# The attention stage of a streaming encoder: where TensorE's spare transposes stand among scores and values

## The reference

```python
def fox_attend(q, k, v, fq, fk, qpos, kpos):
    s = jnp.einsum('bqkgd,bskd->bkgqs', q, k) * (FOX_DH ** -0.5)
    s = s + fq_ - fk[:, :, :, None, :]          # decay between query and key
    s = jnp.where(kpos[None, :] <= qpos[:, None], s, -jnp.inf)
    p = jax.nn.softmax(s, axis=-1)
    o = jnp.einsum('bkgqs,bskd->bqkgd', p, v)
...
    o = o.reshape(b, L, FOX_W) * jax.nn.silu(g)
    return x + gate[:, None, :] * (o @ w_out), ...
```

## Time and profile before

| | us |
|---|---|
| median of three runs | 1787.82 |
| the profiled execution, its own time | 1787.6 |
| its span, first to last instruction | 1785.8 |
| TensorE busy | 1719.3 |
| VectorE, ScalarE, GpSimd busy | 693.5, 564.4, 341.2 |
| the tail in that execution, from 1454 to the end | about 332 |

### The profile page before, as it was taken

How to read it: one execution, slowest core, us unless ns; L and a number is a source line. 1 busy time by engine, 2 the same in 40 slices (tenths; PEclk the granted TensorE clock), 3 DMA queues, 4 the chain that set the end, 5 groups by cost and what they waited for, 6 DMA issues and landing times.

```text
span 1785.8 us, 21820 instructions
## 1 busy us (share of the span) xinstructions
PE 1719.3 (96%) x8461; PEld 1325.1 (74%) x8461; DVE 693.5 (39%) x1421; ACT 564.4 (32%) x924; POOL 341.2 (19%) x409
## 2 busy tenths in 40 slices
PE   3699999999999999999999999999999998999998
PEld 0699998777876666666668888888788866777776
DVE  1654443111134344444533334744552115443432
ACT  2321111111133444444431224425222134344432
POOL 1311111100012222222232125415201000110000
PEclk9999999999999999999999999999999999999999
DMA  9064444452345656556562311332223635332200
GB/s 336 33 222 161 153 159 152 162 183 83 121 148 175 208 183 194 171 187 232 170 235 67 105 48 36 118 106 88 89 92 120 179 136 166 116 103 71 71 25 36
DMA packets 122136, 242.86 MB, mean 136 GB/s; under 512 B 15617, under 2 KB 50589, under 8 KB 121010
## 3 DMA queue, kind: packets, MB, share of 16 engines
q1 hardware_dynamic: 101282, 175.61, 30.7%
q0 software_dynamic: 20752, 65.86, 9.6%
HBM read 170.42 MB, written 70.99 MB: 135 GB/s over the span
## 4 chain that ended last, share of the span: by engine, by line
PE 94%; ACT 1%; DVE 1%; issue 1%; POOL 0%; DVEq 0%; ACTq 0%; POOLq 0%
PE trunk_ps L1053 39%; PE in_ps_o L538 11%; PE in_ps_o L534 11%; PE tail_ps L1906 6%; PE tail_ps L1897 4%; PE tail_ps L1864 3%; PE trunk_ps L1079 3%; PE trunk_ps L1094 3%; PE tail_ps L1874 2%; PE trunk_ps L1089 2%; PE trunk_ps L1155 1%; PE tail_ps L1840 1%; PE in_ps_o L559 1%; PE trunk_ps L1123 1%; PE trunk_ps L1066 1%; PE trunk_ps L1112 1%
## 5 line engine op out<-in xcount | busy, mean ns | idle before, releaser
L1053 PE MATMUL trunk_ps<-w_hi,hT_hi 128*128 128x512 f32 x1008 | 410.4, 407 | 0.0
L1053 PE MATMUL trunk_ps<-w_hi,hT_lo 128*128 128x512 f32 x1008 | 401.1, 398 | 0.0
L1053 PE MATMUL trunk_ps<-w_lo,hT_hi 128*128 128x512 f32 x1008 | 397.2, 394 | 0.0
L1053 PEld LDWEIGHTS trunk_ps<-w_hi,hT_hi 128*128 128x128 f32 x1008 | 189.3, 188 | 59.4 <-issue 17.5
L1053 PEld LDWEIGHTS trunk_ps<-w_lo,hT_hi 128*128 128x128 f32 x1008 | 189.5, 188 | 49.3 <-issue 5.0
L1053 PEld LDWEIGHTS trunk_ps<-w_hi,hT_lo 128*128 128x128 f32 x1008 | 189.2, 188 | 44.5
L203 DVE TENSOR_TENSOR w_lo<-w_raw,w_hi 128x1024 fp32r<-128x1024 f32 x80 | 101.4, 1270 | 298.1 <-ACT w_hi L191 292.2
L534 PE MATMUL in_ps_o<-hT_hi,w_hi 128*128 128x384 f32 x384 | 131.5, 342 | 4.7 <-DVE hT_lo L620 4.7
L534 PE MATMUL in_ps_o<-hT_hi,w_lo 128*128 128x384 f32 x384 | 130.0, 339 | 0.0
L534 PE MATMUL in_ps_o<-hT_lo,w_hi 128*128 128x384 f32 x384 | 130.0, 338 | 0.0
L538 PE MATMUL in_ps_o<-w_hi,hT_hi 128*128 128x512 f32 x288 | 114.4, 397 | 0.0
(11 more groups left out here) (240 smaller groups left out, 2649.7 us busy)
## 6 DMA issues: line engine op xcount, KB each, us to landing
w_raw<-in_a_w_in SPq DMA_DIRECT2D x96, 256.0 KB, 3.0
room<-in_state_ret SPq DMA_DIRECT2D x64, 256.0 KB, 4.0
out_state_sample<-room POOLq DMA_DIRECT2D x64, 256.0 KB, 4.7
room<-in_b_ada_w SPq DMA_DIRECT2D x24, 512.0 KB, 6.2
scratch_qkT<-room POOLq DMA_DIRECT2D x48, 192.0 KB, 2.2
scratch_v<-room POOLq DMA_DIRECT2D x36, 256.0 KB, 2.5
room<-scratch_v SPq DMA_DIRECT2D x36, 256.0 KB, 4.4
scratch_o<-room POOLq DMA_DIRECT2D x36, 256.0 KB, 3.6
```

The source lines that it names most:

```text
L1053: ins = pe.matmul(ps[:, bank, :], h[:, k, t * P:(t + 1) * P], w[:, (C0 + j) % 2, k, :], start=k + m == 0, stop=k == KT - 1 and m == 2)
```

## The change

Two pairs of statements change places, one pair on TensorE and one on VectorE. On TensorE the extras of a unit are issued before `values(u)`. On VectorE `low_part(s, i)` is issued before `output(u)`. Nothing is added or removed; ScalarE, GpSimd and the DMA queues keep their lists, and so does `ring`.

```diff
@@ -1918,9 +1918,9 @@
                 turn_weights(u)
                 if u + 2 < UNITS:
                     scores(u + 2)
-                values(u)
                 for key in extras(s, i):
                     turn(key)
+                values(u)
                 if s:
                     n0 = sum(COUNT[:i])
                     for c, h in ITEMS[n0:n0 + COUNT[i]]:
@@ -2115,9 +2115,9 @@
                 over_sum(u)
                 if u + 2 < UNITS:
                     softmax(u + 2)
-                output(u)
                 if s and i < 2:
                     low_part(s, i)
+                output(u)
                 if s == 0 and i % 2 == 0:
                     split_lo(pr, dve, C0 + 1, 1, i // 2)
```

## The result

The changed kernel takes 1771.95 us (median of six runs, 1767.10 to 1772.52) against 1786.45 us for the kernel before on the same occasions: a ratio of 0.9913, with a 95% interval of 0.9902 to 0.9925. By the profiled executions it is 1772.2 against 1787.6, so 15.4 us less, where 11.9 were forecast. The direction came out as forecast, and so did the places, but for units 8 and 9; the sum was 3.5 us short. Executions of one kernel lie several microseconds apart (1781.11 to 1788.79 before), so the single terms are read from the profiles.

A forecast was written before the change was run, and what follows sets the result against it. TensorE, busy 1719.3 of 1785.8 us, was taken as the bound, so only its idle gaps could count. Minus 6.2, plus 0.3, minus 1.0, 1.8 and 3.2 made minus 11.9: 1776 us, range 1774 to 1778, with rivals 1771.5 to 1783.

The forecast's parts named there:

- units 8 and 9: Step 1, units 0 and 1: longer VectorE chain and an expected fall of the granted clock, plus 0.3 us.
- steps 5 to 8: Second weight group of unit 1 waits less for `low_part`: 0.8 us, four times, minus 3.2 us.
- gaps ahead of the values in steps 1 to 4: Units 2 to 4 of each step: turns fill gaps of 0.33 to 0.35, 0.28, 0.17 and 0.06 us.
- first two units of steps 2 to 4: Second output turn waits for `low_part`, taking back most of the vanished gap: 0.1 us gained per step.
- Step 0: Earlier key turns bring `move`, cast and copy forward; unit 8 begins 6.2 us earlier: minus 6.2 us.
- minus 1.0 becomes plus 0.3: Up to unit 10's values: low clock makes work about 1.7 us longer, some 0.4 of it slack.
- a gain of 1.0 at full clock: Unit 8's start to unit 10's values: 8.1 us after the change against 9.1 before.
- Units 10 to 12 and steps 2 to 4: Turns fill gaps ahead of values: minus 1.0 us in step 1, minus 1.8 us in steps 2 to 4.
- (a): The clock does not fall in step 1: minus 1.3 us more, 1774.6 us; chance 0.18.
- (b): Step 0 gives only half, or the low clock lasts longer: 1779.1 us; chance 0.20.
- (c): Units 0 and 1, steps 1 to 4: TensorE waits for `output` behind `low_part`, 1.6 us each; 1791.2 us; chance 0.04.
- (d): No change: idle time only moves and ScalarE sets the pace, 1787 us; chance 0.05.

The follow-up runs named there:

- early load: Changed kernel with the load of step 1's values tile issued ahead of the last weight quarter: 1772.06 us, ratio 0.9924 to the kernel before.
- filler: Changed kernel with twelve and eight more identity transposes ahead of the values of units 8 and 9: 1768.95 us, ratio 0.9908 to the kernel before.
- query and key turns alone: Kernel before with TensorE's new order only at i of 2 and up in steps 1 to 8, VectorE as before: 1783.10 us, ratio 0.9976.
- last turn moved: Changed kernel with early load and the turn of the last step's first output half ahead of unit 71's values: 1771.93 us, ratio 0.9918 to before.
- no residual addition: Changed kernel without GpSimd's residual addition (line 2015), stores and semaphores kept: 1766.37 us in one run, its tail beginning 4.6 us earlier.
- step 0 alone: Kernel before with TensorE's new order in step 0 only, all else as before: 1781.95 us, ratio 0.9969.

## Where the prediction was right, and which steps failed

The mechanism was right: most of the gain is idle time of TensorE that the turns fill, and `low_part` ahead of `output` lets the weights of steps 5 to 8 go on. What failed are the sizes of four terms, which make nearly all of the 3.5 us. The stretch of units 8 and 9 has the wrong sign (1.1 us, the chain and the low clock both too dear). The gaps ahead of the values in steps 1 to 4 were priced at the gap or less, and a closed gap gives back more (1.0 us). The first two units of steps 2 to 4 were put at almost nothing for a wait that came in one step of three (0.7 us). In steps 5 to 8 `low_part` was started too late (0.6 us).

**Step 0 (forecast -6.2, measured -6.47).** Right, and by its own steps: `move` leads to the next scores, the cast stands ahead of the copy. Unit 2 began 1.26 us nearer to the start of the tail (forecast 1.27), units 4, 6 and 8 3.8, 4.6 and 6.5 us (forecast 3.7, 4.4 and 6.2). The residual gap of about half a microsecond in unit 5 is there (0.5 us, ahead of line 1888).

**Units 8 and 9 (forecast +0.3, measured -0.78).** The step that failed is the sum behind "minus 1.0 becomes plus 0.3". It counts from the start of unit 8 to the values of unit 10: 9.1 us before, 8.1 after at full clock, and 1.3 more for a fall of the clock (1.7 us of longer work less 0.4 of slack), so 9.4. The 9.1 is right, 1485.73 to 1494.81. In the changed kernel it was not 9.4 but 8.37, from 1479.38 to 1487.75. First in the kernel before, then in the changed one:

```profile
1494.81 0.46 PE L1897 MATMUL tail_ps<-room,tail_pT 128*128 128x128 f32 x2 [0.22 <-ACT tail_pT L1995]
```

```profile
1487.75 0.41 PE L1897 MATMUL tail_ps<-room,tail_pT 128*128 128x128 f32 x2
```

Both terms were too dear. The chain takes 7.64 us where the clock held (early load, 1478.40 to 1486.04; the same with filler), not 8.1. The fall of the clock then cost 0.73 us, not 1.3. One reason is the slack: with filler, at full clock, TensorE would have been ready for the values of unit 10 at about 1486.67 (an estimate, the turn's start at 1486.23 and its 0.44 us), and `output` let them start at 1487.39, so the slack is 0.7 us and not 0.4.

The words "a gain of 1.0 at full clock" set a chain at full clock against a kernel that was at 0.50 for 6.8 us of this stretch. That does not enter the sum, since 9.1 is what the kernel before took. But it hides that at full clock in both the new order gains nothing up to unit 10 (6.16 against 6.20 us from unit 8) and loses 0.4 up to unit 11. That the stretch came out at a gain is the clock's doing and in this sense luck: TensorE is at 0.50 from about 1487 to 1493.8 before and from 1483.6 to 1487 after, clock 0.91 instead of 0.83 over the same 20 us. The order of the chain was right: values of unit 9 wait for `output` (0.70 us), behind `low_part`:

```profile
1482.79 0.69 DVE L2093 TENSOR_TENSOR tail_oT_lo<-room,tail_oT_hi 128x512 fp32r<-128x512 f32 x1 [0.69 <-ACT tail_oT_hi L1973]
...
1483.40 0.34 DVE L2070 SCALAR_TENSOR_TENSOR tail_o<-tail_ps,tail_mx,tail_g 128x128 f32<-128x128 f32 x1
...
1483.80 0.80 PE L1897 MATMUL tail_ps<-room,tail_pT 128*128 128x128 f32 x2 [0.70 <-DVE tail_o L2070]
```

**Units 10 to 12 and steps 2 to 4 (forecast -1.0 and -1.8, measured -1.26 and -3.21).** The mechanism was right, two sizes were off. "A gap of 0.39 which a turn of 0.44 fills" was priced at 0.33 to 0.35. A turn that fills the gap gives back all of it, 0.39, and the quicker pair of values and turn 0.05 more, together about the 0.43 measured. In steps 2 to 4 the gaps were priced right (0.28, 0.17 and 0.06) and the 0.07 us beside each left out: 0.35, 0.24 and 0.14 measured. The query and key turns alone gave the same, 1.1 us in units 10 to 12 and 2.2 us in steps 2 to 4, where the forecast has 1.0 and 1.5. And for units 0 and 1 of steps 2 to 4 I took 0.1 us per step, since the second turn waits for `low_part`. That happened only in step 2 (0.78 us waited, 0.03 us gained in the pair); steps 3 and 4 gained 0.57 and 0.38. The -3.21 lies beyond the bound of -2.7 that the forecast gave for steps 2 to 4.

**Steps 5 to 8 (forecast -3.2, measured -3.8).** The mechanism is right: the turn leads, and `low_part` follows the softmax at once, here in step 5.

```profile
1589.33 0.08 DVE L2051 DVE_READ_ACCUMULATOR2_ANT tail_mx<- 128x1 f32 x1
1589.33 0.69 DVE L2093 TENSOR_TENSOR tail_oT_lo<-tail_ps,tail_oT_hi 128x512 fp32r<-128x512 f32 x1
1589.37 1.04 PE L1874 MATMUL tail_ps<-ident,tail_s_sb 128*128 128x128 f32 x5
...
1590.08 0.14 PEld L1874 LDWEIGHTS tail_ps<-ident,tail_s_sb 128*128 128x128 f32 x1 [0.35 <-DVE tail_oT_lo L2093]
```

The remaining wait is hidden within a merged group: step 5's weights take 0.87 us from start to start instead of 0.55, so 0.32 us, close to the 0.38 that the forecast leaves of 1.18. Only step 8's shows in the list, 0.20 us. The 0.6 us more than forecast come from the start of `low_part`, at least in step 5. The forecast put it at the end of the softmax's last record (1601.04 in the earlier trace rows); it started together with that record, 0.08 us sooner, and the fifth transpose followed its end by 0.06 us instead of 0.1 (1590.02 to 1590.08). So from unit 41's start to that transpose are 0.71 us, where the forecast has 0.84.

**The rivals.** (a) The clock fell in the changed kernel's profile and in that of the kernel with the last turn moved, but not in three others with this order in units 8 and 9 (early load, filler, no residual addition), so whether it does in a given run is open; it is worth 0.66 us there, not 1.3. (b) is refuted by step 0. (c), `output` behind `low_part` as the bound, is what VectorE's part does alone, 1.0016, at 0.4 to 0.7 us a step in steps 2 to 4 instead of 1.6 per place; beside TensorE's part it shows once. (d) is refuted. The load lay under VectorE's chain, as forecast; in the kernel with step 0 alone it did not.

What stays open: why the low stretch was shorter in the changed kernel, and what decides whether it comes. The kernel with the early load and the one with the last turn moved issue the same work up to unit 71, and the clock held in the first profile and fell in the second.

## What to carry to other kernels

Work that waits for nothing belongs between the request for a result and its use; first replay one unit from the traces' starts, and price a gap by the distance of the starts, not by the list of waits (0.39 against 0.22 us here; closed, it gave 0.43). Look at who frees the bank, since a filler that needs the result itself fills nothing. Move the consumer on the other engine with it: half of such a change can cost time. And if a stretch contains a low clock, price it against the slack of the new order, and compare both orders at the same clock too: otherwise the clock's share passes for that of the order.

## What the runs showed of the hardware

- A 128x128 VectorE softmax instruction that reads SBUF took 0.96 us while GpSimd's 128x512 addition ran beside it, and 0.35 us with the addition left out; one that reads PSUM took 0.28 us beside it.
- A group of float32 values and a turn behind a wait took 0.65 us from start to start in step 1 and 0.87 in step 2; in the other order, without the wait, 0.60 and 0.80.
- The granted clock fell to 0.50 in units 8 to 10 in seven of the twelve profiles, and in one of two kernels whose work is the same up to there; it cost the kernel before 2.2 us.
